# Dense projections of a hybrid decoder: three token blocks of 384, 384, 320 become 256, 416, 416, and the first block multiplies its high and low activations in one product of 512 columns

## The chip, the cores and the metric

The kernel runs on one core of one Trainium2 chip. The metric is the device time of one execution in microseconds. Three runs of the kernel before took 5048.07, 5056.26 and 5062.81 us, so the median is 5056.26 us. One execution was also recorded by the hardware profiler; its span is 5055.9 us.

## The reference, cut to what matters

Two layers of a decoder trunk process 1088 tokens (1024 of a prompt and 8 x 8 of samples), each a row of 1024 numbers in float32.

```
xn   = rmsnorm(x)                       # x * rsqrt(mean(x*x) + eps) * gain
z    = xn @ w_in                        # 1024 -> 2048 mixer columns + 4 * 1024 gate columns
br_a = short convolution, br_b = convolution of width 31 + layer norm,
br_c = pooling windows 2..16, br_d = gated unit on chunks of 128   # each 256 wide, from z
x    = x + (sum_i sigmoid(gate_i) * (br_i @ w_branch_i)) @ w_out
layer 0: x = x + (silu(xn2 @ wg) * (xn2 @ wu)) @ wd          # dense, 2816 wide
layer 1: x = x + top-2-of-8 experts of the same form, 3584 wide
x    = x + sigmoid(rmsnorm(x) @ ple_w_gate) * (p @ ple_w_proj)
```

The result is a last rmsnorm of x and the states of the mixers.

## The kernel before, in words

Activations lie transposed, channels on partitions and tokens along the free dimension. Every number is held as a high and a low part (fp32r) whose sum is the float32 value: `XHI` and `XLO` for the activations, `WHI` and `WLO` for the weights. A product of two such numbers is three products, high x high, high weight x low activation, low weight x high activation (`product`, lines 699 to 708), all added up in one PSUM bank. The share that is not computed is low x low.

A dense unit (`column_unit`) makes 128 output channels for all 1088 tokens. The tokens go in three blocks, `BLOCKS` of 384, 384 and 320. Per block there are 8 slices of the contraction (KC = 8), each with 3 matmuls, so 24 matmuls to a block and 72 to a unit; each block fills one bank of a ring of six. `open_bank` lets TensorE run at most five blocks ahead of the evictions. There are 168 dense units: 46 of the input projection, 8 of `w_out` and 8 of the last gate in each layer, and 44 of the dense feed-forward. The `w_out` units take `MHI` and `MLO`, the merged branches, in place of `XHI` and `XLO`.

The order of the work on each engine is written out by hand, and each engine does its list in that order. Weights are brought in by SyncE's DMA queue, split into a high part by ScalarE (line 1302) and a low part by VectorE (`convert`, line 1703), three units ahead. VectorE takes each block out of PSUM with one `tensor_tensor` that multiplies by the reciprocal norm `RSTD` of the tokens (lines 1824, 1870, 1878, 2100, 2232, 2242), or, for `w_out`, adds to the residual (line 2212).

Four kinds of place matter besides the plain units:

- `gate_project` (TensorE from line 748, VectorE from line 1830) runs eight steps d = 0 to 7, each a dense unit for a gate and three small branch products (lines 754 to 756, 6 matmuls a block). In step 0 the three gate blocks come first and then the three branch products; in the later steps they alternate. Before the first branch product of a step, TensorE waits until VectorE has made the low part of that step's branch weight (`split_pw`, line 1793), which VectorE does in the step before, ahead of the third block. There are five such stages per layer: br_d, br_a, br_b, br_c and the last gate with the projected embedding (here the embedding stage).
- In the embedding stage VectorE, per block, evicts the gate (line 1824), adds a square into the norm (line 1731), multiplies the branch by the gate (line 2585) and adds the two halves of the residual (lines 2588, 2590); ScalarE takes the sigmoid (line 1346) and the squares (line 1646), and converts the next weight only after the third block.
- Norms: after the first block of some units TensorE does other work, handed in as `between`: the sums of squares over channels (line 732), the spread of the reciprocal norm over partitions (line 744), transposes of states (lines 803, 807). Each waits for VectorE first, and TensorE goes on with the second block only after it.
- The first `w_out` unit of a layer takes slice k as soon as VectorE has made `MLO` of slice k (line 1817); four of the eight slices are made only after the last branch product.

The experts of layer 1 and the second half of the feed-forward (`down`, lines 810 to 823) have loops of their own. `down` also goes over `BLOCKS`.

Of the kernel before, what the change touches and what calls it, by code (L numbers as in the profile page):

```python
# [39 lines left out]
BLOCKS = ((0, 384), (384, 384), (768, 320))  # L40
# [98 lines left out]
def build(nc, A, O):  # L139
# [18 lines left out]
    XHI = sb("XHI", [P, KC, NTOK], F32R)  # L158
    XLO = sb("XLO", [P, KC, NTOK], F32R)
# [6 lines left out]
    T = [sb(f"T{i}", [P, 384]) for i in range(4)]  # L166
    IDF = sb("IDF", [P, P])
    IDR = sb("IDR", [P, P], F32R)
    TRIL = sb("TRIL", [P, P])
# [9 lines left out]
    XHF, XLF = XHI[:].bitcast(F32), XLO[:].bitcast(F32)  # L179
# [3 lines left out]
    MLO = at("MLO", [P, KC, NTOK], F32R, PH)  # L183
    MHI = at("MHI", [P, KC, NTOK], F32R, PH + 34816)
# [61 lines left out]
    def mo(name, shape, dt=F32):  # L246
# [85 lines left out]
        "xnew_ready", "y_full", "v_out", "par_ready", "rw_loaded", "nrs_loaded", "rtok_clear", "row_squares", "scale_ready", "ids_ready", "mask_ready", "list_ready", "rows_written", "squared", "summed", "sums_taken", "weights_ready", "spacer")}  # L332
# [78 lines left out]
    def _(sp):  # L411
# [20 lines left out]
        def load_x(block):  # L432
            t0, m = BLOCKS[block]
# [98 lines left out]
    def _(g):  # L532
# [4 lines left out]
        g.memset(IDF[:], 0.0).then_inc(S["pool_own"], 1)  # L537
        g.memset(TRIL[:], 1.0).then_inc(S["pool_own"], 1)
        g.wait_ge(S["pool_own"], 2)
        g.affine_select(out=IDF[:], in_=IDF[:], compare_op=ALU.not_equal, fill=1.0, base=0, pattern=[[-1, P]],  # L540
# [139 lines left out]
    def _(pe):  # L680
# [29 lines left out]
        def blocks_of(HI, LO, splits=None, between=()):  # L710

            slot = unit.n % HL
            for j, (t0, n) in enumerate(BLOCKS):
                b = open_bank()
                product(b, n, slot, lambda k: HI[:, k, t0:t0 + n], lambda k: LO[:, k, t0:t0 + n],
                        (lambda k: splits(j, k)) if splits else None).then_inc(q.next(), 1)
                if j < len(between):
                    between[j]()

        def column_unit(HI, LO, splits=None, between=()):  # L720

            use()
            blocks_of(HI, LO, splits, between)
            unit.n += 1
# [14 lines left out]
        def spread():  # L739

            pe.wait_ge(S["diag_ready"], diag.take())
            for j, (t0, n) in enumerate(BLOCKS):
                b = misc_bank()
                pe.matmul(PS[:, b, 0:n], ONES[:], T[j][:, 0:n], start=True, stop=True).then_inc(m.next(), 1)
# [3 lines left out]
        def gate_project(ready, count, Y, splits=None, between=()):  # L748

            def branch(t0, n):  # L750
                b = open_bank()
                wh, wl = PWH[pw.n % 2], PWL[pw.n % 2]
                for k in range(2):
                    pe.matmul(PS[:, b, 0:n], wh[:, k, :], Y[0][:, k, t0:t0 + n], start=(k == 0), stop=False)  # L754
                    pe.matmul(PS[:, b, 0:n], wh[:, k, :], Y[1][:, k, t0:t0 + n], start=False, stop=False)  # L755
                    ins = pe.matmul(PS[:, b, 0:n], wl[:, k, :], Y[0][:, k, t0:t0 + n], start=False, stop=(k == 1))  # L756
                ins.then_inc(q.next(), 1)

            for d in range(KC):
                use()  # L760
                slot = unit.n % HL
                if d == 0:
                    blocks_of(XHI, XLO, splits, between)
                    pe.wait_ge(S[ready], count)
                    pe.wait_ge(S["pw_lo"], pw.n + 1)
                    for t0, n in BLOCKS:
                        branch(t0, n)
                else:
                    for t0, n in BLOCKS:
                        b = open_bank()  # L770
                        product(b, n, slot, lambda k: XHI[:, k, t0:t0 + n], lambda k: XLO[:, k, t0:t0 + n]).then_inc(q.next(), 1)
                        if t0 == 0:
# [53 lines left out]
        pe.wait_ge(S["consts"], 3)  # L826
# [3 lines left out]
        for block, (t0, n) in enumerate(BLOCKS):  # L830
# [16 lines left out]
        for l in range(DEPTH):  # L847

            def p_columns(tiles):
                pe.wait_ge(S[f"p_loaded{l}"], 16 * NT)  # L850
                for c in range(2):
                    for t0, n in BLOCKS:
                        b = misc_bank()
                        for j in range(t0 // P, -(-(t0 + n) // P)):
                            w = tokens(j)
                            ins = pe.transpose(PS[:, b, j * P - t0:j * P - t0 + w], tiles[j][0:w, c * P:(c + 1) * P], IDF[0:w, 0:w])
                        ins.then_inc(m.next(), 1)

            if l:
                column_unit(XHI, XLO, splits=lambda j, k: W_MIX1 + KC * j + k + 1, between=(stats, spread))  # L860
                column_unit(XHI, XLO)
            else:
                use()
                slot = unit.n % HL
                for j, (t0, n) in enumerate(BLOCKS):
                    pe.wait_ge(S["evicted"], KC * (j + 1))
                    b = open_bank()
                    product(b, n, slot, lambda k: XHI[:, k, t0:t0 + n], lambda k: XLO[:, k, t0:t0 + n]).then_inc(q.next(), 1)
                unit.n += 1
                column_unit(XHI, XLO, between=(spread,))  # L870
# [24 lines left out]
            for _ in range(3):  # L895
                column_unit(XHI, XLO)
# [18 lines left out]
            column_unit(XHI, XLO)  # L915
            gate_project("br_d", l + 1, U_SPLIT, between=(lambda: states_out(GLU, YB, PB),))
            for _ in range(4):
                column_unit(XHI, XLO)
            column_unit(XHI, XLO, between=(lambda: states_out(ZA, YA, PA),))
            column_unit(XHI, XLO)  # L920
# [10 lines left out]
            column_unit(XHI, XLO, between=(channel_sums,))  # L931
            pe.wait_ge(S["lnsq_ready"], l + 1)
            token_sums(SQB[:, 0, :], SQB[:, 1, :])
            column_unit(XHI, XLO, between=(spread,))
# [11 lines left out]
            for d in range(KC):  # L946
                merged = (W_FFN if l == 0 else W_MOE) - 3 * KC - KC
                column_unit(MHI, MLO, splits=(lambda j, k: merged + k + 1) if d == 0 else None)
            if l == 0:
                hs = Count()  # L950

                def step(kind, g, first=False):
                    if kind == "GU":
                        for u in range(4):
                            if first and u == 0:
                                column_unit(XHI, XLO, splits=lambda j, k: W_FFN - 3 * KC + 3 * k + j + 1, between=(stats, spread))
                            else:
                                column_unit(XHI, XLO)
# [296 lines left out]
            else:  # L1255
                gate_project("p_ready", 2, P_SPLIT[1], splits=lambda j, k: hs.at(hs.n + min(6 * j + 6, 2 * NT)), between=(spread,))
# [15 lines left out]
    def _(act):  # L1272
# [110 lines left out]
        for t0, n in BLOCKS:  # L1383
# [8 lines left out]
        for block, (t0, n) in enumerate(BLOCKS):  # L1392
# [298 lines left out]
    def _(dve):  # L1691
# [20 lines left out]

        pending = []
# [35 lines left out]
        def diagonals():  # L1749

            for j, (t0, n) in enumerate(BLOCKS):
# [10 lines left out]
        def spread_rstd():  # L1762

            for t0, n in BLOCKS:
# [54 lines left out]
        def gates(d, j, pulls=0):  # L1819

            t0, n = BLOCKS[j]
            ps = main_ready()
            t = T[j] if d == 0 else T[req.n % 2]
            v.do(dve.tensor_tensor(t[:, 0:n], ps[:, 0:n], RSTD[:, t0:t0 + n], ALU.mult), q)
# [36 lines left out]
        def padded_unit(buf, pad, c, times=False, tmp=[0]):  # L1861

            convert()
            for j, (t0, n) in enumerate(BLOCKS):
                ps = main_ready()
                ps_r = ps
                if times:
                    t = T[2 + tmp[0] % 2]
                    tmp[0] += 1
                    v.do(dve.tensor_tensor(t[:, 0:n], ps[:, 0:n], RSTD[:, t0:t0 + n], ALU.mult), q)  # L1870
# [3 lines left out]
                    v.sync()  # L1874
                else:
                    ds = pieces(j, buf[:, c, :], pad)
# [24 lines left out]
        def p_columns(whole, parts):  # L1901

            for c in range(2):
                for t0, n in BLOCKS:
# [18 lines left out]
        v.do(dve.tensor_copy(IDR[:], IDF[:]))  # L1923
# [13 lines left out]
        for j, (t0, n) in enumerate(BLOCKS):  # L1937
# [16 lines left out]
        for l in range(DEPTH):  # L1954
# [18 lines left out]
            for c in range(2):  # L1973
                convert()
                for t0, n in BLOCKS:
                    ps = main_ready()
                    v.do(dve.tensor_tensor(UB[:, c, t0:t0 + n], ps[:, 0:n], RSTD[:, t0:t0 + n], ALU.mult), q)
# [117 lines left out]
            for c in range(2):  # L2095
                convert()
                for t0, n in BLOCKS:
                    ps = main_ready()
                    t = T[2]
                    v.do(dve.tensor_tensor(t[:, 0:n], ps[:, 0:n], RSTD[:, t0:t0 + n], ALU.mult), q)  # L2100
# [26 lines left out]
            for t0, n in BLOCKS:  # L2127
# [65 lines left out]
            for d in range(KC):  # L2193
# [26 lines left out]
            if l == 0:  # L2220
# [5 lines left out]
                def step(kind, g, last=False):  # L2226
                    if kind == "GU":
                        for f in range(2):
                            convert()
                            for t0, n in BLOCKS:  # L2230
                                ps = main_ready()
                                v.do(dve.tensor_tensor(GS[:, f, t0:t0 + n], ps[:, 0:n], RSTD[:, t0:t0 + n], ALU.mult), q)
                                v.sync()
                                dve.sem_inc(req.next(), 1)
                        for f in range(2):
                            convert()
                            for j, (t0, n) in enumerate(BLOCKS):
                                ps = main_ready()
# [3 lines left out]
                                v.do(dve.tensor_tensor(t, ps[:, 0:n], RSTD[:, t0:t0 + n], ALU.mult), q)  # L2242
# [28 lines left out]
                per = {conv: 12, q: 72, req: 12, split: 12, sreq: 12, v.own: 12}  # L2271
# [386 lines left out]
```

## Time and profile before

| what | value |
|---|---|
| time, three runs | 5048.07, 5056.26, 5062.81 us; median 5056.26 us |
| profiled execution | span 5055.9 us; what lies around the span is not recorded for it, and the median of the runs is 0.4 us above the span |
| TensorE matmul busy | 4935.7 us, 98% of the span, 33281 matmuls |
| VectorE busy | 3231.2 us, 64% |
| ScalarE busy | 1745.1 us, 35% |
| mean granted TensorE clock | 0.987 |

Matmuls of the records overlap: one of 384 columns is shown as 0.33 us long, while the next one starts 0.17 us after it. What a matmul costs in a stream is therefore read from the distance between starts, not from its length. A granted clock of 1.00 is the upper of the two levels, 2.4 GHz; 0.50 is the lower, 1.2 GHz. In rows of the timeline, the bracket at the end tells how long the engine had been idle and what ended it; "DVEq L1795" is VectorE's queue signalling at line 1795.

### The profile page before, as it was taken

Reading aid. Unit: us, or ns where it says so; the run is one execution under the profiler, and the core shown is the slowest. Engines: PE = TensorE matmul, PEld = TensorE weight load, DVE = VectorE, ACT = ScalarE, POOL = GpSimd, SP = SyncE. Lnnn points to the kernel's source line nnn. Section 1 sums busy time; section 2 is a strip of 40 time slices with the busy share of each in tenths; the row PEclk is TensorE's granted clock in tenths of the full one; section 3 lists DMA queues with packets and bytes.
Section 4 is the critical chain, followed back from the end, with each engine's and each line's share of the span. In section 5 each row is a group of like instructions: output and inputs, shape, how many; then the busy total and the mean of one; then the engine's idle time right before and its main releaser. Section 6 shows DMA issues by size and latency. Waiting matters only on the chain.

```text
span 5055.9 us, 87486 instructions
## 1 busy us (share of the span) xinstructions
PE 4935.7 (98%) x33281; PEld 4878.9 (96%) x33282; DVE 3231.2 (64%) x5248; ACT 1745.1 (35%) x2666; POOL 302.4 (6%) x441
## 2 busy tenths in 40 slices
PE   8999999999999999999979999999999999999998
PEld 8999999999998999999979999999999999999988
DVE  4666656444546656766557777666667787876655
ACT  3323322111113433233234444333334444443333
POOL 2000002111112000000020000000000000000030
PEclk9999999999999999999989999999999999999999
DMA  3111111111111111111025554444446555554431
GB/s 107 45 47 41 42 39 42 51 41 41 50 42 44 42 46 52 48 41 42 30 90 197 178 178 165 157 141 161 153 150 197 188 194 186 197 192 153 142 134 43
DMA packets 397853, 521.94 MB, mean 103 GB/s; under 512 B 13192, under 2 KB 353654, under 8 KB 397512
## 3 DMA queue, kind: packets, MB, share of 16 engines
q1 hardware_dynamic: 358320, 459.63, 27.5%
q10 hardware_dynamic: 29272, 33.08, 1.9%
q0 software_dynamic: 9920, 24.85, 1.7%
q8 instruction: 193, 3.16, 0.3%
q14 instruction: 148, 1.21, 0.1%
HBM read 494.91 MB, written 22.60 MB: 102 GB/s over the span
## 4 chain that ended last, share of the span: by engine, by line
PE 81%; issue 9%; DVE 5%; DMA 2%; ACT 1%; DVEq 0%; POOL 0%; ACTq 0%; SPq 0%; POOLq 0%
PE PS L705 20%; PE PS L707 19%; PE PS L706 19%; PE PS L818 5%; PE PS L820 5%; PE PS L819 5%; PE PS L754 1%; PE PS L755 1%; PE PS L756 1%; DMA WRAW<-in_moe_w_gate 1%; DVE EACC L2509 1%; PE PS L1244 1%; DVE WLO L1703 1%; ACT WHI L1302 1%; DVE XSL L2458 0%
## 5 line engine op out<-in xcount | busy, mean ns | idle before, releaser
L1703 DVE TENSOR_TENSOR WLO<-WRAW,WHI 128x1024 fp32r<-128x1024 f32 x866 | 1060.0, 1225 | 417.9 <-ACT WHI L1302 298.3
L705 PE MATMUL PS<-XHI,WHI 128*128 128x384 f32 (+1 forms) x3648 | 1200.9, 329 | 14.4 <-DVE XLO L1960 8.3
L707 PE MATMUL PS<-XHI,WLO 128*128 128x384 f32 (+1 forms) x3648 | 1196.1, 328 | 0.0
L1302 ACT ACTIVATE WHI<-WRAW 128x1024 fp32r<-128x1024 f32 x866 | 899.3, 1051 | 858.8 <-PE PS L820 603.4
L706 PE MATMUL PS<-XLO,WHI 128*128 128x384 f32 (+1 forms) x3648 | 1195.2, 328 | 0.0
L705 PE MATMUL PS<-XSH,WHI 128*128 128x232 f32 (+6 forms) x3584 | 1059.1, 296 | 14.5 <-DVEq L2461 12.0
L707 PE MATMUL PS<-XSH,WLO 128*128 128x232 f32 (+6 forms) x3584 | 1055.6, 295 | 0.0
L706 PE MATMUL PS<-XSL,WHI 128*128 128x232 f32 (+6 forms) x3584 | 1054.1, 294 | 0.0
L705 PEld LDWEIGHTS PS<-XHI,WHI 128*128 128x128 f32 x3648 | 689.9, 189 | 16.6 <-issue 9.0
L705 PEld LDWEIGHTS PS<-XSH,WHI 128*128 128x128 f32 x3584 | 678.8, 189 | 16.6 <-DVEq L2461 13.6
L706 PEld LDWEIGHTS PS<-XLO,WHI 128*128 128x128 f32 x3648 | 689.7, 189 | 0.9
L707 PEld LDWEIGHTS PS<-XHI,WLO 128*128 128x128 f32 x3648 | 689.4, 189 | 0.0
L707 PEld LDWEIGHTS PS<-XSH,WLO 128*128 128x128 f32 x3584 | 679.0, 189 | 0.0
L706 PEld LDWEIGHTS PS<-XSL,WHI 128*128 128x128 f32 x3584 | 678.7, 189 | 0.0
L818 PE MATMUL PS<-EHI,WHI 128*128 128x232 f32 (+6 forms) x1792 | 532.0, 297 | 4.8 <-DVE EACC L2509 3.0
L820 PE MATMUL PS<-EHI,WLO 128*128 128x232 f32 (+6 forms) x1792 | 525.0, 293 | 0.0
L819 PE MATMUL PS<-ELO,WHI 128*128 128x232 f32 (+6 forms) x1792 | 524.5, 293 | 0.0
L2509 DVE TENSOR_TENSOR EACC<-PS,EACC 128x336 f32<-128x336 f32 x832 | 372.7, 499 | 43.1 <-PE PS L820 15.9
L818 PEld LDWEIGHTS PS<-EHI,WHI 128*128 128x128 f32 x1792 | 338.8, 189 | 7.2 <-DVE EACC L2509 3.8
L1346 ACT ACTIVATE T<-T 128x384 f32<-128x384 f32 (+1 forms) x240 | 121.9, 508 | 640.7 <-DVEq L1826 640.4
L819 PEld LDWEIGHTS PS<-ELO,WHI 128*128 128x128 f32 x1792 | 338.9, 189 | 0.0
L820 PEld LDWEIGHTS PS<-EHI,WLO 128*128 128x128 f32 x1792 | 338.8, 189 | 0.0
(408 smaller groups left out, 5810.6 us busy)
## 6 DMA issues: line engine op xcount, KB each, us to landing
WRAW<-in_moe_w_gate SPq DMA_DIRECT2D x112, 1024.0 KB, 5.0
WRAW<-in_moe_w_up SPq DMA_DIRECT2D x112, 1024.0 KB, 5.0
WRAW<-in_moe_w_down SPq DMA_DIRECT2D x112, 1024.0 KB, 4.9
WRAW<-in_w_in SPq DMA_DIRECT2D x48, 1024.0 KB, 5.2
WRAW<-in_ffn_w_gate SPq DMA_DIRECT2D x11, 1024.0 KB, 5.3
WRAW<-in_ffn_w_up SPq DMA_DIRECT2D x11, 1024.0 KB, 5.3
WRAW<-in_ffn_w_down SPq DMA_DIRECT2D x11, 1024.0 KB, 4.9
expert_rows<-YT ACTq DMA_DIRECT2D x18, 512.0 KB, 3.8
```

The lines of the kernel that those rows point to most:

```text
L705: pe.matmul(PS[:, bank, 0:n], wh, hi(k), start=(k == 0), stop=False)
L706: pe.matmul(PS[:, bank, 0:n], wh, lo(k), start=False, stop=False)
L707: ins = pe.matmul(PS[:, bank, 0:n], wl, hi(k), start=False, stop=(k == KC - 1))
L754: pe.matmul(PS[:, b, 0:n], wh[:, k, :], Y[0][:, k, t0:t0 + n], start=(k == 0), stop=False)
L755: pe.matmul(PS[:, b, 0:n], wh[:, k, :], Y[1][:, k, t0:t0 + n], start=False, stop=False)
L818: pe.matmul(PS[:, b, 0:n], WHI[s][:, d, :], hi[:, f, t0:t0 + n], start=(f == 0), stop=False)
L819: pe.matmul(PS[:, b, 0:n], WHI[s][:, d, :], lo[:, f, t0:t0 + n], start=False, stop=False)
L820: ins = pe.matmul(PS[:, b, 0:n], WLO[s][:, d, :], hi[:, f, t0:t0 + n], start=False, stop=(f == 1))
L1302: act.activation(WHI[halves.n % HL][:], raw_view(tile % RAW, half, kind), ACT.Copy).then_inc(halves.next(), 1)
L1346: serve(lambda: act.activation(t[:, 0:n], t[:, 0:n], ACT.Sigmoid))
L1703: v.do(dve.tensor_tensor(WLO[s][:], raw_view(conv.n // 2 % RAW, conv.n % 2, kind), WHI[s][:].bitcast(F32), ALU.subtract), conv)
L2509: v.do(dve.tensor_tensor(a, ps[:, 0:CAP], a, ALU.add), q)
```

## The change

`BLOCKS` becomes 256, 416, 416 for all that is tied to a dense unit, `down` and the branch products included. `TILED` keeps the old cuts for the transposes at the start and for the norms. The high and low activations become the two planes of one tensor (`X2`, and `M2` for `w_out`). In the first block each slice is two matmuls in place of three: the high weight with both planes, 2 x 256 = 512 columns, and the low weight with the high plane, 256 columns, added to that plane's half of the bank. So the bank holds two parts, and VectorE adds them: a `tensor_reduce` over the pair, then the multiplication by `RSTD` in SBUF (`scaled`); for `w_out` two additions. The other blocks are as before, 24 matmuls each. The tiles `T` grow to 416 columns; the identity matrix shares its memory between its two types to make room.

```
-BLOCKS = ((0, 384), (384, 384), (768, 320))
+BLOCKS = ((0, 256), (256, 416), (672, 416))
+TILED = ((0, 384), (384, 384), (768, 320))
+HALF = BLOCKS[0][1]
...
-    XHI = sb("XHI", [P, KC, NTOK], F32R)
-    XLO = sb("XLO", [P, KC, NTOK], F32R)
+    X2 = sb("X2", [P, 2, KC, NTOK], F32R)
+    XHI, XLO = X2[:, 0], X2[:, 1]
...
+        def pair_product(bank, slot, X, hi, splits=None):
+            both = PS[:, bank, 0:2 * HALF].rearrange("p (h t) -> p h t", h=2)
+            for k in range(KC):
+                if splits is not None:
+                    pe.wait_ge(S["split_done"], splits(k))
+                pe.matmul(both, WHI[slot][:, k, :], X[:, :, k, 0:HALF], start=(k == 0), stop=False)
+                ins = pe.matmul(PS[:, bank, hi * HALF:(hi + 1) * HALF], WLO[slot][:, k, :], X[:, hi, k, 0:HALF], start=False, stop=(k == KC - 1))
+            return ins
...
+        def scaled(j, out):
+            t0, n = BLOCKS[j]
+            ps = main_ready()
+            if j == 0:
+                v.do(dve.tensor_reduce(out, ps.rearrange("p (h t) -> p t h", h=2), AXX, ALU.add), q)
+                v.sync()
+                v.do(dve.tensor_tensor(out, out, RSTD[:, t0:t0 + n], ALU.mult))
+            else:
+                v.do(dve.tensor_tensor(out, ps[:, 0:n], RSTD[:, t0:t0 + n], ALU.mult), q)
...
-                    v.do(dve.tensor_tensor(t, ps[:, 0:n], XHF[:, d, t0:t0 + n], ALU.add), q)
+                    if j == 0:
+                        v.do(dve.tensor_tensor(t, ps[:, 0:n], XHF[:, d, t0:t0 + n], ALU.add))
+                        v.sync()
+                        v.do(dve.tensor_tensor(t, ps[:, n:2 * n], t, ALU.add), q)
+                    else:
+                        v.do(dve.tensor_tensor(t, ps[:, 0:n], XHF[:, d, t0:t0 + n], ALU.add), q)
```

## Rows read from the trace of the kernel before

**Rows 1.** The page: busy us (share of the span) and instructions of each engine

```profile
PE 4935.7 (98%) x33281; PEld 4878.9 (96%) x33282; DVE 3231.2 (64%) x5248; ACT 1745.1 (35%) x2666; POOL 302.4 (6%) x441
```

**Rows 2.** Busy time by stretch: PE, PEld, DVE, ACT, POOL, clock, DMA share

```profile
1100.00:1200.00 100.00, 100.00 (x608) 100.00 (x607) 41.70 (x67) 17.37 (x27) 15.45 (x26) 1.00 0.17 52
...
1660.00:1770.00 110.00, 104.57 (x630) 103.53 (x629) 70.38 (x127) 44.64 (x89) 0.00 (x0) 1.00 0.12 38
```

**Rows 3.** Timeline of PE, feed-forward: one dense unit and the next one's start

```profile
1107.17 0.34 PE L705 MATMUL PS<-XHI,WHI 128*128 128x384 f32 x1
...
1115.52 0.31 PE L705 MATMUL PS<-XHI,WHI 128*128 128x320 f32 x1
...
1119.03 0.34 PE L705 MATMUL PS<-XHI,WHI 128*128 128x384 f32 x1
```

**Rows 4.** Timeline of PE: 256 columns read as two ranges of 128, twelve starts

```profile
69.92 0.28 PE L879 MATMUL PS<-WHI,XHI 128*128 128x256 f32 x1
...
71.36 0.28 PE L879 MATMUL PS<-WHI,XHI 128*128 128x256 f32 x1
```

**Rows 5.** Timeline of PE: 512 columns read as four ranges of 128

```profile
4859.16 0.39 PE L1240 MATMUL PS<-XLO,IDR 128*128 128x512 f32 x1
4859.40 0.83 PE L1244 MATMUL PS<-DG,YG 128*128 128x128 f32 x6
```

**Rows 6.** Groups by line of DVE: busy us, mean ns, idle before and releaser

```profile
L1824 DVE TENSOR_TENSOR T<-PS,RSTD 128x384 f32<-128x384 f32 x160 | 88.7, 554 | 86.5 <-PE PS L707 83.4 <-DVE XNEW L2590 1.9 <-DVE T L1824 0.2
...
L1824 DVE TENSOR_TENSOR T<-PS,RSTD 128x320 f32<-128x320 f32 x80 | 39.3, 491 | 68.3 <-PE PS L707 64.6 <-DVE PWL L1793 2.5 <-PE PS L756 0.2
...
L2019 DVE TENSOR_TENSOR V<-V,LNG 128x256 f32<-128x256 f32 x16 | 5.5, 420 | 0.1
...
L2403 DVE TENSOR_REDUCE LROW<-LCMP 14x32 f32<-14x416 f32 x1 | 0.6, 574 | 0.0
```

**Rows 7.** Timeline of DVE, embedding stage of layer 0: last additions of three steps

```profile
1694.49 0.49 DVE L2590 TENSOR_TENSOR XNEW<-XNEW,XLO 128x320 f32<-128x320 f32 x1
...
1711.21 0.49 DVE L2590 TENSOR_TENSOR XNEW<-XNEW,XLO 128x320 f32<-128x320 f32 x1
...
1724.54 0.49 DVE L2590 TENSOR_TENSOR XNEW<-XNEW,XLO 128x320 f32<-128x320 f32 x1
```

**Rows 8.** Waits of DVE from 1662 to 1770: us in total, times, longest

```profile
DVE T L1824 <- PE PS L707: 0.3, 2, 0.2
```

**Rows 9.** Timeline of PE, embedding stage of layer 1: first branch products of steps

```profile
4959.73 0.44 PE L754 MATMUL PS<-PTMHI,PWH 128*128 128x384 f32 x1 [0.57 <-DVEq L1795]
...
4975.41 0.44 PE L754 MATMUL PS<-PTMHI,PWH 128*128 128x384 f32 x1 [0.57 <-DVEq L1795]
```

**Rows 10.** Timeline of DVE up to br_a's and br_b's weight for step 1

```profile
332.14 0.49 DVE L2100 TENSOR_TENSOR T<-PS,RSTD 128x320 f32<-128x320 f32 x1 [1.69 <-PE PS L707]
...
349.94 0.42 DVE L1793 TENSOR_TENSOR PWL<-PWR,PWH 128x256 fp32r<-128x256 f32 x1
...
506.64 0.42 DVE L1793 TENSOR_TENSOR PWL<-PWR,PWH 128x256 fp32r<-128x256 f32 x1
```

**Rows 11.** Timeline of PE: step 1's first branch product, br_a, br_b, br_d

```profile
350.89 0.34 PE L754 MATMUL PS<-YAHI,PWH 128*128 128x384 f32 x1
...
507.18 0.45 PE L754 MATMUL PS<-YBHI,PWH 128*128 128x384 f32 x1
...
1907.64 0.45 PE L754 MATMUL PS<-UHI,PWH 128*128 128x384 f32 x1 [1.27 <-DVEq L1795]
```

**Rows 12.** The chain that ended last, layer 0, at the first w_out unit

```profile
731.99 4.91 DVE MLO L1817 x4
```

**Rows 13.** Timeline of DVE, then PE: last square added, sums of squares, feed-forward

```profile
832.25 0.48 DVE L1731 TENSOR_TENSOR SQS<-SQS,T 128x320 f32<-128x320 f32 x1
...
833.53 2.04 PE L732 MATMUL PS<-ONES,SQS 128*128 128x1 f32 x18
```

**Rows 14.** Timeline of PE, start of layer 1: the spread of the norm

```profile
1786.12 2.37 PE L744 MATMUL PS<-T,ONES 128*128 128x384 f32 x6 [0.89 <-DVEq L1760]
```

More of the change, by code:

```diff
@@ L165, in build @@
     RSTD = sb("RSTD", [P, NTOK])
-    T = [sb(f"T{i}", [P, 384]) for i in range(4)]
-    IDF = sb("IDF", [P, P])
+    T = [sb(f"T{i}", [P, WIDE]) for i in range(4)]
     IDR = sb("IDR", [P, P], F32R)
+    IDF = IDR[:].bitcast(F32)
+    EYE = T[3][:, 0:P]
     TRIL = sb("TRIL", [P, P])
@@ L432, in load_x @@
         def load_x(block):
-            t0, m = BLOCKS[block]
+            t0, m = TILED[block]
             for j in range(t0 // P, -(-(t0 + m) // P)):
@@ L768, in gate_project @@
                 else:
[L769 to L772, printed above, removed]
+                    for j, (t0, n) in enumerate(BLOCKS):
+                        block_of(j, slot, X2, 0)
+                        if j == 0:
                             pe.wait_ge(S["pw_lo"], pw.n + 1)
@@ L829, in _ @@
         pe.transpose(PS[:, b, 0:7 * KC], NRS[:], IDF[0:7 * KC, 0:7 * KC]).then_inc(m.next(), 1)
-        for block, (t0, n) in enumerate(BLOCKS):
+        for block, (t0, n) in enumerate(TILED):
             tiles = range(t0 // P, -(-(t0 + n) // P))
@@ L851, in p_columns @@
                 for c in range(2):
-                    for t0, n in BLOCKS:
+                    for t0, n in TILED:
                         b = misc_bank()
@@ L864, in _ @@
                 slot = unit.n % HL
-                for j, (t0, n) in enumerate(BLOCKS):
+                for j in range(len(BLOCKS)):
                     pe.wait_ge(S["evicted"], KC * (j + 1))
-                    b = open_bank()
-                    product(b, n, slot, lambda k: XHI[:, k, t0:t0 + n], lambda k: XLO[:, k, t0:t0 + n]).then_inc(q.next(), 1)
+                    block_of(j, slot, X2, 0)
                 unit.n += 1
-                column_unit(XHI, XLO, between=(spread,))
+                column_unit(X2, between=(spread,))
             use(2)
@@ L1255, in _ @@
             else:
-                gate_project("p_ready", 2, P_SPLIT[1], splits=lambda j, k: hs.at(hs.n + min(6 * j + 6, 2 * NT)), between=(spread,))
+                gate_project("p_ready", 2, P_SPLIT[1], splits=lambda j, k: hs.at(hs.n + 2 * -(-sum(BLOCKS[j]) // P)), between=(spread,))
         stats()
@@ L1391, in _ @@
         act.wait_ge(S["rtok_clear"], 1)
-        for block, (t0, n) in enumerate(BLOCKS):
+        for block, (t0, n) in enumerate(TILED):
             tiles = range(t0 // P, -(-(t0 + n) // P))
@@ L1749, in diagonals @@
         def diagonals():
-            for j, (t0, n) in enumerate(BLOCKS):
+            for j, (t0, n) in enumerate(TILED):
                 whole = n // P
@@ L1762, in spread_rstd @@
         def spread_rstd():
-            for t0, n in BLOCKS:
+            for t0, n in TILED:
                 ps = misc_ready()
@@ L1903, in p_columns @@
             for c in range(2):
-                for t0, n in BLOCKS:
+                for t0, n in TILED:
                     ps = misc_ready()
@@ L1936, in _ @@
         dve.sem_inc(S["par_ready"], 1)
-        for j, (t0, n) in enumerate(BLOCKS):
+        for j, (t0, n) in enumerate(TILED):
             for c in range(KC):
@@ L2126, in _ @@
             diagonals()
-            for t0, n in BLOCKS:
+            for t0, n in TILED:
                 ps = misc_ready()
@@ L2270, in _ @@
                 cs = [conv, q, req, split, sreq, v.own]
-                per = {conv: 12, q: 72, req: 12, split: 12, sreq: 12, v.own: 12}
+                per = {conv: 12, q: 72, req: 12, split: 12, sreq: 12, v.own: 20}
                 with dve.Fori(0, FFN_LOOP) as i:
```

97 lines of the change are left out of this document (51 added, 46 removed).

## The prediction

> **What bounds the kernel now.** I read the page's busy times first, then stretches, then single units. TensorE is busy 98% of the span and VectorE 64% [rows 1], so the path runs through TensorE unless a stretch says otherwise. In the feed-forward TensorE has no gap in 100 us at the full clock, while VectorE works 42 of them [rows 2]; VectorE's additions are hidden there. In the embedding stage of layer 0 TensorE is busy only 104.6 of 110 us [rows 2], and there VectorE waits for TensorE's products only 0.3 us in all [rows 8]: the chain VectorE to ScalarE and back sets the pace. The reader should keep these two apart, since the change speeds TensorE and slows VectorE.
>
> **What the matmuls cost.** In a dense unit 48 matmuls of 384 columns take 8.35 us, 174.0 ns from start to start, and 24 of 320 take 3.51 us, 146.3 ns; the unit takes 11.86 us [rows 3]. At clock 1.00 (2.4 GHz) a column is 0.4167 ns: 160.0 and 133.3 ns, and 14.0 and 12.9 ns are left. With 256 columns in two ranges of 128, twelve starts take 1.44 us, 120.0 ns, of which 13.3 are left [rows 4]. So a matmul costs its columns plus about 13.3 ns, whatever its width, and reading two ranges costs nothing.
>
> The columns do not change: 8 x (512 + 256) in the first block are the 24 x 256 that it would have had. What changes is the count, 64 matmuls a unit in place of 72. Eight fixed parts are 107 ns. The 512-column matmul isn't in the dense units before; the nearest row, four ranges of 128 and followed by another kind of matmul, shows 0.24 us [rows 5] against 226.7 ns by the rule above. I take 228, near the two-range row since the new read has two ranges; the other end, 240, stays for the range. A unit then costs 8 x 228 + 8 x 120.0 + 48 x 186.7 = 11.74 us against 26112 x 0.4167 + 72 x 13.3 = 11.84: 0.096 us less. By the ends it is 0.107 and 0.000. Sixteen of the 168 units lie in the two embedding stages, which another chain paces (below). The rest give 152 x 0.096 = **14.6 us** gained (0 to 16.2). The second feed-forward half and the branch products keep count and columns: nothing.
>
> The Trainium skill, "TensorE: Matmul & The Clock Gate", section "Back-to-back issue gap", puts the gap of a warm matmul at N / 2.4 ns plus 2.5 ns. By that, 168 x 8 = 1344 matmuls fewer would give 3.4 us. The trace disagrees at these widths (13 to 14 ns). What this would leave is the second rival below.
>
> **What VectorE pays.** An eviction of 384 takes 554 ns, one of 320 491 [rows 6], so 0.984 ns an element, and 416 takes 585 (estimate). A 256-wide multiplication in SBUF takes 420, a reduction of 416 elements 574 [rows 6]; for 512 in PSUM I estimate 668, with 420 (no slower than 256) and 1340 (the two halves, 1 KB apart, read at half rate) as ends. Per unit: before 554 + 554 + 491 = 1.60 us; after 668 + 30 to the dependent start + 420 + 585 + 585 = 2.29: **0.69 us more**, 0.44 to 1.36. ScalarE's sums stay, as all its work is linear in the same 1088 tokens. Where TensorE has no gap this costs nothing; it is paid in these places:
>
> 1. Embedding stage, layer 0. Two steps take 1694.49 to 1724.54, 30.05 us [rows 7]; TensorE would need 2 x (11.86 + 2.96) = 29.6. The chain gate, sigmoid, additions, square, weight conversion and next gate runs without a gap. Seven steps x 0.69 = 4.8. At the start, blocks 1 and 2 stand behind the norm's matmuls and grow by 128 tokens: 24 x 128 x 0.4167 ns = 1.3. Sum **6.1**.
> 2. Embedding stage, layer 1. Steps follow at 15.68 us, and TensorE waits for the branch weight [rows 9]. Four such steps x (0.69 + 0.07 for signals) and 0.4 at step 1: **3.4**. The last steps convert no weight and have slack.
> 3. Step 1 of the mixer stages. VectorE makes the branch weight after three gates, so this wait is the tightest. In br_a it is anchored at the eviction 332.14 that waited for TensorE; the weight is there at 349.94 + 0.42, and TensorE comes at 350.89 [rows 10, 11]: 0.5 us of slack, 0.4 past the signal. TensorE's way from the same anchor gets shorter by 1.5 (block 0 is 2.78 instead of 4.18 us, and 0.1), VectorE's longer by 0.8: a new wait of 1.9 per layer. In br_b the weight comes at 507.06 and TensorE at 507.18 [rows 10, 11], no slack; the anchor lies behind an earlier first block, so TensorE's way shrinks only 0.2, while VectorE's has two reductions: 1.5 per layer. br_d in layer 1 waits already 1.27 [rows 11] and gets 0.8 more, in layer 0 0.7. Sum 3.8 + 3.0 + 1.5 = **8.3**. From step 2 on the weights are several us early; br_c is early throughout. Everything queued behind this wait on TensorE is late with it.
>
> **What the shorter first block uncovers.** TensorE takes its list in order, and some waits are hidden by block 0, which falls from 4.18 to 2.78 us. The squares of the feed-forward norm end at 832.73 and TensorE comes at 833.53 [rows 13]: 0.8 of slack against 1.4 less cover and 0.4 longer chain (416 evicted in place of 320): 1.0. In the first `w_out` unit VectorE makes four slices in 4.91 us [rows 12] while TensorE has only block 0 to do; 128 tokens more are left behind it (1.1) and the chain starts 0.3 later: 1.4 a layer, 2.8. At the start of layer 1 the spread already waits 0.89 [rows 14], and the block behind it grows by 96 tokens: 0.9. The routing of the experts and the end of the kernel hang on a last block that is 416 in place of 320: 0.5 and 0.65. Sum **5.9**. The start of the kernel, the experts and SyncE's and GpSimd's queues are not touched: they use the old cuts.
>
> **Sum.** -14.6 + 6.1 + 3.4 + 8.3 + 5.9 = +9.1 us on the profiled execution's span of 5055.9: **5065 us**, 0.18% more. The median of the three runs, 5056.26, stands 0.4 above that span, so I add nothing for what lies around it. With a measurement that tells about 0.3% (15 us) from no change, the forecast is "no change, a little slower".
>
> **Rivals.**
>
> - *The saving comes whole, the waits do not.* VectorE catches up inside the stages (its background additions are pulled at fixed points and end sooner), and of the 23.7 us of losses only the embedding stage of layer 0 stays. Then 5055.9 - 16.2 + 4.8 = 5044, or 5040 without most of that too. For it: from step 2 on the mixer stages have slack. Against: step 1 comes before it, and rows 7 and 8 show a chain without gaps.
> - *The pair product saves nothing* (the other side: slower). Place: each of the 168 first blocks. If the 512-column matmul costs 240 ns as in rows 5, the eight fixed parts are given back (8 x 13.3) and the losses stand alone: 5055.9 + 23.7 = 5080. It decides from 8 x 5.1 ns on, so from about 233 ns: there the sum passes 15 us over. For it: the only 512-column rows. Against: rows 4, where ranges cost nothing and the fixed part is the same as for narrower ones. By the rule of the Trainium skill above (same page and section) it would be 5076.
> - *The reduction runs at half rate* over its two halves: 0.67 us more a unit, 11 more steps of the embedding stages (7.4) and about as many reductions in the step-1 chains (6): 5078. For it: no row reads pairs so far apart. Against: the 574 ns for 416 elements.
>
> **How the numbers follow.** Forecast 0.50, first rival 0.15, second 0.22, third 0.13. The forecast's own range is 5053 to 5070. Slower by over 0.3% (above 5071): most of the second and third, and 0.02 of the forecast, 0.30. Faster (below 5041): two thirds of the first, 0.10. The rest, 0.60, within. The range 5042 to 5081 takes in the ends of the 512-column price and most of the reduction's.
>
> **What would show it.** Starts of a dense unit 11.74 us apart where TensorE has no gap, 512-column starts 228 ns from the next, reductions near 0.67 us. Step 1's first branch products in br_a, br_b and br_d with VectorE's queue as releaser, together some 8 us more idle. Embedding stage of layer 0 about 5 us longer, 15.7 us a step. A sums-of-squares matmul that waits 1 us in the feed-forward. The prediction is wrong if the 512-column matmul is above 233 ns, if a reduction takes over 1 us, or if the step-1 waits are not there.

## The result, and the profile after

The changed kernel takes 5083.24 us (median of four runs, 5079.87 to 5091.60), the kernel before 5057.59 in the runs beside it: a ratio of 1.0055, 95% interval 1.0043 to 1.0066. It is slower by 25.7 us. The forecast was 5065, with a range that ends at 5081. The profiled execution of the changed kernel has a span of 5078.3 us, 22.4 more than before.

The page's busy times after:

```profile
PE 4941.6 (97%) x31937; PEld 4801.9 (95%) x31938; DVE 3333.7 (66%) x5416; ACT 1744.7 (34%) x2666; POOL 295.3 (6%) x441
```

Against [rows 1] TensorE has exactly the 1344 matmuls fewer that the change promised, and is busy 5.9 us *more*. VectorE pays 102.5 us. So matmuls have gone, but not their time. Where it stayed is seen in a stretch of the feed-forward without gaps. The timeline of PE after, two dense units: first matmul of the first block, of the second block, and of the next unit.

```profile
1113.65 0.40 PE L720 MATMUL PS<-X,WHI 128*128 128x512 f32 x1
...
1116.43 0.35 PE L709 MATMUL PS<-X,WHI 128*128 128x416 f32 x1
...
1125.50 0.39 PE L720 MATMUL PS<-X,WHI 128*128 128x512 f32 x1
...
1128.31 0.36 PE L709 MATMUL PS<-X,WHI 128*128 128x416 f32 x1
...
1137.42 0.40 PE L720 MATMUL PS<-X,WHI 128*128 128x512 f32 x1
```

The two units take 11.85 and 11.92 us; before it was 11.86 [rows 3], the forecast 11.74. The first blocks take 2.78 and 2.81 us, as forecast (8 x 348 ns = 2.78). The 48 matmuls of 416 columns take 9.07 and 9.11 us, 189.0 and 189.8 ns each, where 186.7 was forecast. That is most of the difference; in the second unit the first block gives another 0.03.

VectorE's groups by line after (busy us, mean ns, idle before); L1738 adds the halves, L1740 multiplies, L1742 evicts 416 columns:

```profile
L1742 DVE TENSOR_TENSOR T<-PS,RSTD 128x416 f32<-128x416 f32 x228 | 134.8, 591 | 215.6 <-PE PS L711 206.3 <-DVE PWL L1824 3.5 <-DVE XNEW L2623 2.3
...
L1738 DVE TENSOR_REDUCE T<-PS 128x256 f32<-128x512 f32 x114 | 78.0, 684 | 1.5 <-PE PS L721 1.1 <-DVE XNEW L2623 0.4
...
L1740 DVE TENSOR_TENSOR T<-T,RSTD 128x256 f32<-128x256 f32 x114 | 48.8, 428 | 4.0
```

684, 428 and 591 ns stand against 668, 420 and 585 of the estimate. Three waits of PE after (total us, times, longest), to be read beside [rows 9 to 14]:

```profile
PE PS L776 <- DVEq L1826: 13.3, 11, 2.2
...
PE PS L720 <- DVE M L1848: 5.6, 8, 1.6
...
PE PS L754 <- DVEq L2253: 1.0, 1, 1.0
```

L776 is the first branch product behind its weight, L720 the first `w_out` units, L754 the sums of squares of the feed-forward norm. The wait of the branch products was, before:

```profile
PE PS L754 <- DVEq L1795: 4.0, 5, 1.3
```

It grew as forecast, but mostly elsewhere: of the 13.3 us after, 4.5 are at step 1 of br_a, br_b and br_d (1.27 before) and 8.8 in the embedding stages (2.75 before). At step 1 some 8 us more were forecast, and 3.2 came.

### The profile page after: what moved, and what is told of

Same layout as the page of the kernel before. It is cut to its first block, busy times and chain, and to the rows that moved or that the text cites. A ratio compares the mean times of both kernels' runs of the same rounds, so it can differ in the third digit from the quotient of the medians.

```text
span 5078.3 us, 84998 instructions
## 1 busy us (share of the span) xinstructions
PE 4941.6 (97%) x31937; PEld 4801.9 (95%) x31938; DVE 3333.7 (66%) x5416; ACT 1744.7 (34%) x2666; POOL 295.3 (6%) x441
## 4 chain that ended last, share of the span: by engine, by line
PE 48%; issue 8%; DVE 4%; DMA 2%; ACT 1%; DVEq 0%; POOL 0%; ACTq 0%; POOLq 0%; SPq 0%
PE PS L709 10%; PE PS L710 10%; PE PS L711 10%; PE PS L839 3%; PE PS L840 3%; PE PS L841 3%; PE PS L720 2%; PE PS L721 1%; PE PS L776 1%; PE PS L1264 1%; PE PS L778 1%; PE PS L777 1%; DMA WRAW<-in_moe_w_gate 1%; DVE EACC L2542 0%; DMA WRAW<-in_moe_w_up 0%
## 5 line engine op out<-in xcount | busy, mean ns | idle before, releaser
L709 PE MATMUL PS<-X,WHI 128*128 128x416 f32 x2432 | 860.0, 354 | 0.0
L710 PE MATMUL PS<-X,WHI 128*128 128x416 f32 x2432 | 856.1, 352 | 0.0
L711 PE MATMUL PS<-X,WLO 128*128 128x416 f32 x2432 | 855.3, 352 | 0.0
L709 PEld LDWEIGHTS PS<-X,WHI 128*128 128x128 f32 x2432 | 458.9, 189 | 8.3 <-issue 0.6
L710 PEld LDWEIGHTS PS<-X,WHI 128*128 128x128 f32 x2432 | 458.9, 189 | 4.9 <-issue 0.6
L711 PEld LDWEIGHTS PS<-X,WLO 128*128 128x128 f32 x2432 | 458.7, 189 | 4.4
L720 PE MATMUL PS<-X,WHI 128*128 128x512 f32 x1216 | 442.4, 402 | 14.8 <-DVE X L1992 7.5
L2542 DVE TENSOR_TENSOR EACC<-PS,EACC 128x336 f32<-128x336 f32 x832 | 373.4, 500 | 42.9 <-PE PS L841 15.8
L1366 ACT ACTIVATE T<-T 128x416 f32<-128x416 f32 (+1 forms) x240 | 121.7, 507 | 659.8 <-DVEq L1856 659.5
L721 PE MATMUL PS<-X,WLO 128*128 128x256 f32 x1216 | 345.2, 284 | 0.0
```

The costliest lines, as they stand in the source:

```text
L709: pe.matmul(PS[:, bank, 0:n], wh, hi(k), start=(k == 0), stop=False)
L710: pe.matmul(PS[:, bank, 0:n], wh, lo(k), start=False, stop=False)
L711: ins = pe.matmul(PS[:, bank, 0:n], wl, hi(k), start=False, stop=(k == KC - 1))
L720: pe.matmul(both, WHI[slot][:, k, :], X[:, :, k, 0:HALF], start=(k == 0), stop=False)
L721: ins = pe.matmul(PS[:, bank, hi * HALF:(hi + 1) * HALF], WLO[slot][:, k, :], X[:, hi, k, 0:HALF], start=False, stop=(k == KC - 1))
L1366: serve(lambda: act.activation(t[:, 0:n], t[:, 0:n], ACT.Sigmoid))
```

## The experiments

The table gives the time from the first matmul of one dense unit to that of another, read from the timeline of PE of one profiled execution each, in us. "Adds" is VectorE's addition of the halves.

| stretch | before | after | e1 cuts alone | e2 three + adds | e3 pair, no adds | e4 pair last | e7 pair hidden |
|---|---|---|---|---|---|---|---|
| two feed-forward units | 23.72 | 23.77 | 23.92 | 23.92 | 23.77 | 23.77 | 23.77 |
| first `w_out` unit, layer 0 | 15.05 | 18.40 | 18.61 | 18.80 | 18.89 | 15.33 | 15.34 |
| the same, layer 1 | 16.07 | 18.68 | 18.49 | 18.97 | 19.13 | 15.35 | 15.35 |
| first feed-forward unit | 16.08 | 17.27 | 18.90 | 18.84 | 20.39 | 17.58 | 17.54 |
| br_a, step 1, layer 0 | 14.84 | 16.64 | 15.83 | 16.57 | 15.88 | 16.26 | 14.97 |
| br_b, step 1, layer 0 | 15.00 | 15.44 | 14.85 | 15.45 | 14.84 | 15.90 | 15.60 |
| embedding stage, layer 0, steps 1 to 7 | 113.11 | 118.76 | 113.38 | 118.78 | 113.36 | 120.23 | 114.32 |
| embedding stage, layer 1, steps 0 to 6 | 112.67 | 116.02 | 113.19 | 116.23 | 113.20 | 115.93 | 112.13 |
| experts (code unchanged) | 2338.44 | 2339.28 | 2344.99 | 2336.68 | 2342.73 | 2341.56 | 2336.38 |

The last row varies by 8.6 us among kernels with the same code there; medians are not fine enough to read a single term from them, the stretches are.

**e1, the cuts alone.**

```
-            if j == 0:
-                ins = pair_product(b, slot, X, hi, splits)
-            else:
+            if True:
                 t0, n = BLOCKS[j]
                 ins = product(b, n, slot, ...)
```

and the same for VectorE's addition.

> The changed kernel's blocks of 256, 416, 416, but with 24 ordinary matmuls of 256 in the first block and no addition on VectorE. It isolates the cuts. The trace of the changed kernel shows starts 118.7 ns apart at 256 columns, 189.1 at 416 and 232.6 at 512; the line through 256 and 512 is 4.8 ns + 0.445 ns a column, and 264, 288, 312, 328, 336 and 416 columns lie within 1 ns of it. Theory L (a matmul costs by its columns at 0.445 ns and only 4.8 ns besides): three blocks of any widths cost the same, so a dense unit takes 11.86 to 11.93 us as before, and what is lost is what the shorter first block uncovers, without VectorE's additions: some 11 us (4.5 at the first w_out units with their clock, 1.8 at step 1 of br_a, 1.3, 1.1, 1.0, 0.8, 0.8 at the other places): about 5069 us. Theory F of the prediction (13.3 ns a matmul, 0.4167 ns a column): unit 11.84, the same 5069. Rival W (the width 416 is dear by itself): units 0.07 to 0.12 us longer, 152 of them: 5080 to 5087.

Measured: 5086.55 us, ratio 1.0057 (1.0043 to 1.0071). Two units' starts in the feed-forward, timeline of PE:

```profile
1117.87 0.28 PE L709 MATMUL PS<-X,WHI 128*128 128x256 f32 x1
...
1141.79 0.28 PE L709 MATMUL PS<-X,WHI 128*128 128x256 f32 x1
```

23.92 us for two: 11.96 a unit, 0.10 more than before with the same columns and the same 72 matmuls. So theory L, which I had read out of the trace of the changed kernel after the result, falls, the prediction's flat 13.3 ns (F) falls with it, and rival W stands as far as the units go: these cuts with 416 columns cost by themselves. e5 below shows that the width alone doesn't make the price. The expected 5069 was missed. The rows of the embedding stages are back to within 0.6 us of before: what was lost there is VectorE's addition. br_a's step 1 keeps 1.0 of its 1.8 us (the shorter first block), and 0.8 goes with the addition. The first `w_out` units keep their loss. The first feed-forward unit takes 1.6 us longer than in the changed kernel: its granted clock is at half for some 3.3 us (0.89 from 840 to 855 us; 1.00 in the changed kernel).

**e2, three matmuls of 256 into the two halves, with the addition.**

```
-                pe.matmul(both, WHI[slot][:, k, :], X[:, :, k, 0:HALF], start=(k == 0), stop=False)
+                pe.matmul(part(hi), WHI[slot][:, k, :], X[:, hi, k, 0:HALF], start=(k == 0), stop=False)
...
+                ins = pe.matmul(part(1 - hi), WHI[slot][:, k, :], X[:, 1 - hi, k, 0:HALF], ...)
```

> The changed kernel, but in the first block the 512-column matmul is replaced by two of 256 columns into the two halves of the bank; VectorE adds the halves as in the changed kernel. 72 matmuls a unit again. It isolates the count. Theory L: 8 x (3 x 118.7 - 350.1) = 0.05 us more a unit, 152 units outside the embedding stages: 7 us slower than the changed kernel, about 5090. Theory F: 8 x 13.3 ns = 0.107 us a unit, 16 us slower, 5099. Rival (the 512-column matmul costs as much as two): no difference, 5083.

Measured: 5095.28 us, ratio 1.0081 (1.0068 to 1.0095). 41.0 us above its runs of before, where the changed kernel is 25.7 above its own: 15 us, with some 6 of uncertainty on each. The units say it more sharply: 23.92 against 23.77 for two, 0.075 a unit, between L (0.05) and F (0.107). The pair product does save time; 152 units make 11.4 us.

**e3, the pair product without the addition.** The product of the high weight and the low activation stays in the bank and out of the result.

```
-            if j == 0:
-                v.do(dve.tensor_reduce(out, ps.rearrange("p (h t) -> p t h", h=2), AXX, ALU.add), q)
...
+            if True:
                 v.do(dve.tensor_tensor(out, ps[:, 0:n], RSTD[:, t0:t0 + n], ALU.mult), q)
```

> The changed kernel, but VectorE takes only one half of the first block's bank out (the half that holds both products of the high activation; the product of the high weight and the low activation is left out of the result), with one multiplication as before. It isolates VectorE's additions. If the prediction's terms for VectorE hold (4.8 in the embedding stage of layer 0, 3.4 in that of layer 1, and of step 1's 8.3 the part that is not the shorter block, some 3): 11 us faster than the changed kernel, about 5072. If the additions are hidden and the losses are the cuts' alone: 5083.

Measured: 5074.49 us, ratio 1.0037 (1.0025 to 1.0049); about 5 us less against its own runs of before than the changed kernel, where 11 were expected. By stretches the expectation holds: 5.4 and 2.8 us in the embedding stages, 0.8 and 0.6 at step 1 of br_a and br_b in layer 0. Its experts took 3.5 us longer than the changed kernel's, its first feed-forward unit 3.1 and its first `w_out` units 0.9. In the first feed-forward unit the clock accounts for it: 0.77 from 832 to 847 us, 1.00 in the changed kernel, so 6.9 us at half, worth 3.4. The waits of PE:

```profile
PE PS L776 <- DVEq L1822: 6.3, 9, 1.0
```

6.3 us for 13.3: half of that wait goes with the addition.

**e4, the short block last.**

```
-BLOCKS = ((0, 256), (256, 416), (672, 416))
+BLOCKS = ((0, 416), (416, 416), (832, 256))
+PAIR = 2
```

> Blocks of 416, 416, 256 with the pair product and VectorE's addition in the last block. Same matmuls in every unit as the changed kernel, but the first block is longer than before (24 x 189 = 4.54 us for 4.18) and covers the norms, the first w_out unit and step 1. Theory L with losses from the cover: the uncovered places and their low clock are gone (about 14 us of the changed kernel's 25.6), step 1's waits shrink by some 2 us, VectorE's additions in the embedding stages stay (8 us), units as in the changed kernel: 5062 us, 5057 to 5067. Theory F: 5050, since the units would gain their 14.6 us as well. If the order of the blocks doesn't matter: 5083.

Measured: 5073.46 us, ratio 1.0035 (1.0022 to 1.0049), 19.1 above before. The cover is given back where expected: the first `w_out` units are at 15.33 and 15.35. But the first feed-forward unit still loses (17.58 us for 16.08 before, 17.27 after; the clock is 0.89 from 835 to 850 us), step 1 of br_a and br_b still loses (16.26 and 15.90), and the embedding stage of layer 0 grew to 120.23. So the order of the blocks was worth 6.4 us in the first `w_out` units (against after) and 2.5 in the embedding stage of layer 0 with its step 0 and the start of layer 1 together, and nothing in the units; the expected 5062 was missed, since it took nearly all losses but VectorE's in the embedding stages for covered.

**e5, the price by width.** A program of its own: 48 matmuls of each width, like those of a block.

> Nothing of the reference is computed: streams of matmuls like a block's (24 with the weights of 8 slices, two products with the high and one with the low weight, all into one bank), of 128 to 512 columns, first with no other engine at work, then with VectorE and ScalarE busy in SBUF. It measures the price of a matmul by width, by itself. Theory L: 4.8 ns + 0.445 ns a column: 256 columns 118.7 ns, 320 147, 384 176, 416 190, 448 204, 480 218, 512 233, whether one range or two planes 34.8 KB apart, and in both stretches. Theory F: 13.3 ns + 0.4167 ns: 120, 147, 173, 187, 200, 213, 227. Rival (the steeper slope comes of the other engines' reads and writes): by F in the quiet stretch, by L in the busy one. Rival (the two planes cost): 2 x 256 some 6 ns above one range of 512.

Measured: no difference between the quiet and the busy stretch. First matmul of each stream of 48, timeline of PE, quiet stretch; the distance of two streams' first rows by 48 is the price. 139.38 is the 25th of 512 columns; 165.45 is the first of 24 that read two planes of 256; from 170.94 on come pair products:

```profile
81.50 0.31 PE L129 MATMUL PS<-X,WHI 128*128 128x320 f32 x1
...
88.54 0.32 PE L129 MATMUL PS<-X,WHI 128*128 128x352 f32 x1
...
96.22 0.34 PE L129 MATMUL PS<-X,WHI 128*128 128x384 f32 x1
...
104.54 0.35 PE L129 MATMUL PS<-X,WHI 128*128 128x416 f32 x1
...
113.58 0.36 PE L129 MATMUL PS<-X,WHI 128*128 128x448 f32 x1
...
123.49 0.38 PE L129 MATMUL PS<-X,WHI 128*128 128x480 f32 x1
...
133.89 0.40 PE L129 MATMUL PS<-X,WHI 128*128 128x512 f32 x1
...
139.38 0.39 PE L129 MATMUL PS<-X,WHI 128*128 128x512 f32 x1
...
144.82 0.35 PE L129 MATMUL PS<-X,WHI 128*128 128x416 f32 x1
...
153.78 0.28 PE L146 MATMUL PS<-X,WLO 128*128 128x256 f32 x1
...
165.45 0.40 PE L146 MATMUL PS<-X,WLO 128*128 128x512 f32 x1
...
170.94 0.39 PE L138 MATMUL PS<-X,WHI 128*128 128x512 f32 x1
...
173.75 0.40 PE L138 MATMUL PS<-X,WHI 128*128 128x512 f32 x1
```

320, 352 and 384 columns cost 146.7, 160.0 and 173.3 ns (the last is 104.54 - 96.22 by 48): 13.3 above 0.4167 ns a column. 512 costs 227.7, 14.4 above. Those are theory F's numbers, nearly so at 512 (226.7). But 416 costs 188.3 (15.0 above), 448 costs 206.5 (19.8), 480 costs 216.7 (16.7). Theory L fails here. And the width alone doesn't set the price: two more blocks of 416, behind the 512 and reading the tokens from 256 and from 672 as the kernel's blocks do, take 8.96 us (144.82 to 153.78), 186.7 ns each, the price by F. Both figures come again in the busy stretch. In the units of the kernel and of e6, where they follow a block of 256 columns, blocks of the same tokens take 188 to 190. What the price hangs on besides the width was not tested further. The last two rows are eight slices of the pair product: 2.81 us, 351 ns a slice; three of 256 at 120.0 are 360. It saves 9 ns of the 13.3. Two planes as one read of 512 cost what one range of 512 does (the first 24 matmuls take 5.49 us in either stream), so the planes are not dear; in the pair the 512 is followed 236 ns later, its 256 only 117.

**e6, whole units, nothing else at work.**

> Nothing of the reference is computed: streams of matmuls with no other engine at work, first single widths between those measured (264 to 504 columns in steps of 8 to 40), then whole dense units, four of each kind: 384/384/320; 256/416/416, 256/320/512 and 256/352/480, each with an ordinary first block and with the pair product. The widths alone showed 13.3 ns over the columns at 256, 320, 352, 384 and 512, but 13.3 to 15.0 at 416, 20.0 at 448, 16.8 at 480, and a pair at 352.7 ns for three 256-column matmuls at 360.0. Theory W (price by width, dear at 416 to 480; the pair saves 7 ns a slice): units of 11.86 for 384/384/320; 11.93 ordinary and 11.87 with the pair for 256/416/416; 11.85 and 11.79 for 256/320/512; 11.9 and 11.85 for 256/352/480. Theory F of the prediction: 11.84, 11.84 and 11.74 whatever the cut. Theory L (a slope of 0.445 ns and 4.8 ns fixed) has already failed: 320 and 384 lie 13.3 above their columns; it would give 11.97 for every ordinary cut.

Measured, first matmul of each kind, four units apart, timeline of PE: 384/384/320; 256/416/416 ordinary, then pair; 256/320/512 ordinary, then pair; 256/352/480 ordinary, then pair.

```profile
196.43 0.34 PE L113 MATMUL PS<-X,WHI 128*128 128x384 f32 x1
...
243.84 0.28 PE L113 MATMUL PS<-X,WHI 128*128 128x256 f32 x1
...
291.68 0.40 PE L122 MATMUL PS<-X,WHI 128*128 128x512 f32 x1
...
339.22 0.28 PE L113 MATMUL PS<-X,WHI 128*128 128x256 f32 x1
...
386.66 0.39 PE L122 MATMUL PS<-X,WHI 128*128 128x512 f32 x1
...
433.86 0.28 PE L113 MATMUL PS<-X,WHI 128*128 128x256 f32 x1
...
481.81 0.40 PE L122 MATMUL PS<-X,WHI 128*128 128x512 f32 x1
```

By four: 11.85, 11.96, 11.89, 11.86, 11.80, 11.99 us; the last kind, 256/352/480 with the pair, takes 11.87. This is the kernel's own table (11.86, 11.96 in e1, 11.885 after) with no other engine running: the unit's price is TensorE's alone. 256/320/512 with the pair product would save 0.06 a unit against before. It was not tried in the kernel: its four `T` tiles of 512 columns need 1.5 KB a partition more, and the tiles of 416 had already taken the room that was made.

**e7, the pair product only where VectorE is hidden.**

```
-                        block_of(j, slot, X2, 0)
+                        block_of(j, slot, X2, 0, pair=(ready != "p_ready" and d > 1))
```

and an ordinary product in step 0, with e4's blocks. `ready != "p_ready"` leaves out the embedding stages, `d > 1` step 1 of the mixer stages.

> Blocks of 416, 416, 256, the pair product and its addition in the last block, but an ordinary product in the two embedding stages and in steps 0 and 1 of the mixer stages, where VectorE's chain sets the pace. If the losses of the kernel with the pair in the last block are VectorE's chain there (10.4 us in the steps of the embedding stages, some 2 to 4 at step 1) and the price of 416 columns (everywhere, 0.08 us a unit where the pair is taken back, 32 units, 2.6 us): 5073 - 13 + 3 = 5063 us, still slower than before. If the losses in these stages come from the order of the blocks instead: 5073 to 5076.

Measured: 5060.43 us, ratio 1.0007 (0.9997 to 1.0016): no difference from before. The embedding stages are back at 114.32 and 112.13 us, so e4's loss there was the addition, not the order of the blocks. The largest losses are gone (smaller ones stay: the first feed-forward unit 1.5 us, step 1 of br_b 0.6) and the pair's saving is spent on the blocks of 416, so about nothing is left on either side. No version tried beats the kernel before.

## Why the prediction was wrong, point by point

Predicted terms against the same stretches of the profiled executions (after minus before, us):

| term | predicted | measured |
|---|---|---|
| dense units | -14.6 (152 units) | -0.8 (the 118 units in stretches without other terms; predicted for these -11.3) |
| embedding stage, layer 0 | +6.1 | +6.8 (steps 1 to 7 +5.65, step 0 +1.16) |
| embedding stage, layer 1 | +3.4 | +3.4 |
| step 1 of the mixer stages | +8.3 | +4.0 (br_a 1.80 + 1.73, br_b 0.44 + 0.44, br_d 0.58 - 0.98) |
| uncovered by the shorter block | +5.9 | +10.0 (first `w_out` 3.35 + 2.62, feed-forward 1.20, layer 1 1.17, experts 0.84, end 0.83) |
| first units of br_b | none | -3.1 (-1.6 and -1.5) |
| start, and end of the feed-forward | none | +2.2 |

But for rounding, the right column adds up to the 22.4 us between the two spans. The first row alone, 13.8 us off, accounts for the miss of 13.3 (22.4 for 9.1). That the four losses add up to 24.2 for 23.7 is luck: step 1 came 4.3 short, and the uncovered waits 4.1 over, in good part through the clock (below).

**The step that failed** is "So a matmul costs its columns plus about 13.3 ns, whatever its width", used at 416. It held at every width it was taken from (256, 320, 384) and, alone, nearly at 512 (14.4). At 416 the fixed part is 15.7 and 16.5 in the two feed-forward units shown above (189.0 and 189.8 ns), at least 2.4 ns more than taken, 48 times a unit: 0.115 us, more than the whole saving of 0.096. Alone it was 15.0 in one pair of blocks and 13.3 in another (e5), so the rule gave a price that 416 can have, but not the one that it has in these units. Nothing in the prediction bounded that price: the estimate 186.7 for 416 stood without ends, although no row of before had that width, while the ends were spent on the 512-column matmul. The trace of before could have given ends. Its experts have streams of other widths, 24 matmuls between two rows, timeline of PE before:

```profile
2648.11 0.28 PE L705 MATMUL PS<-XSH,WHI 128*128 128x264 f32 x1
...
2651.03 0.28 PE L705 MATMUL PS<-XSH,WHI 128*128 128x264 f32 x1
...
4532.76 0.31 PE L705 MATMUL PS<-XSH,WHI 128*128 128x328 f32 x1
...
4536.38 0.31 PE L705 MATMUL PS<-XSH,WHI 128*128 128x328 f32 x1
```

264 columns take 121.7 ns and 328 take 150.8: 11.7 and 14.2 over their columns. By 14.2 the saving of a unit is 0.05 us, half of what was forecast. The 512-column matmul cost 231 to 233 ns with a following 256 at 117 to 119: 350 a pair for 348 in the sum. By e1 and e2 the change's two halves are +0.10 us a unit for the cuts and -0.075 for the pair.

**The second rival** gave nearly the right time (5080 for a span of 5078.3 and a median of 5083.24) with half the right reason, and so partly by luck: nothing was saved in the units, but not because the 512-column matmul costs 240 ns. Its threshold of 233 ns was nearly met; by e2 the pair product still saves. The first rival falls with the saving. The third falls too: the reduction took 684 ns, near the 668 of the forecast and far from 1340.

**Step 1** was mis-sized at br_b and br_d. br_a came as worked out: a wait of 1.57 us at the branch product for 1.9. Timeline of PE, layer 0:

```profile
353.22 0.39 PE L776 MATMUL PS<-YAHI,PWH 128*128 128x256 f32 x1 [1.57 <-DVEq L1826]
```

br_b had 1.5 predicted and got 0.44, and e3, without the addition, none; the estimate charged two reductions to a chain with no slack, and which part of that was too much was not tested. br_d of layer 1 waited 1.27 before [rows 11]; that stretch became 0.98 shorter.

**The embedding stage** went nearly as read. Last additions of two steps that lie two apart, timeline of DVE after, beside [rows 7]:

```profile
1705.15 0.59 DVE L2623 TENSOR_TENSOR XNEW<-XNEW,X 128x416 f32<-128x416 f32 x1
...
1737.26 0.59 DVE L2623 TENSOR_TENSOR XNEW<-XNEW,X 128x416 f32<-128x416 f32 x1
```

Two steps take 32.1 us for 30.05; 31.4 was forecast. e1 and e3, with no addition, are both at 113.4 for the seven steps. These two steps lost 1.0 us each where 0.69 was forecast, all seven 5.65 for 4.8. Not all of the loss need be the chain: behind a new wait of 2.21 us at a branch product the granted clock fell too (0.89 from 1750 to 1765 us). How much that cost was not tested.

**The first `w_out` unit** lost 3.35 and 2.62 where 1.4 and 1.4 were worked out. Three of the four waits, timeline of PE in layer 0 (the fourth is 0.20):

```profile
734.82 0.50 PE L720 MATMUL PS<-M,WHI 128*128 128x512 f32 x1 [1.62 <-DVE M L1848]
...
736.02 0.78 PE L720 MATMUL PS<-M,WHI 128*128 128x512 f32 x1 [0.59 <-DVE M L1848]
...
737.22 0.79 PE L720 MATMUL PS<-M,WHI 128*128 128x512 f32 x1 [0.21 <-DVE M L1848]
```

From the second on the matmuls are 0.78 us long: the clock has fallen to half behind the wait of 1.62. By windows of 15 us (PE, PEld, DVE, ACT, POOL busy, granted clock, DMA) from 735 on: after, then before, then e4:

```profile
735.00:750.00 15.00, 14.01 (x56) 12.29 (x57) 7.59 (x11) 3.67 (x7) 0.00 (x0) 0.77 0.22 71
```

```profile
735.00:750.00 15.00, 14.18 (x83) 13.54 (x83) 9.28 (x15) 4.34 (x8) 0.00 (x0) 1.00 0.22 71
```

```profile
735.00:750.00 15.00, 14.22 (x73) 12.97 (x74) 9.96 (x15) 4.97 (x9) 0.00 (x0) 1.00 0.22 71
```

A mean of 0.77 over 15 us is 6.9 us at half, worth 3.4: about the whole loss, while the four waits together grew by 0.6 only (2.6 us for 2.0). Before, in layer 0, the waits were 0.78 and three of 0.41, and the clock stayed; in e4, with 24 matmuls of 416 in the first block, the first wait was 1.23 and it stayed too. But the length of the first wait doesn't settle it: in layer 1 before, the waits began with 0.79, 0.41 and 0.41 again, and there the clock did fall. Layer 1, before and then after:

```profile
2482.00:2497.00 15.00, 14.59 (x77) 13.89 (x77) 8.37 (x14) 4.57 (x8) 0.00 (x0) 0.89 0.21 71
```

```profile
2497.00:2512.00 15.00, 14.22 (x60) 12.86 (x59) 6.97 (x12) 2.33 (x5) 0.00 (x0) 0.77 0.22 71
```

So that unit took 16.07 us before, 1.0 more than in layer 0, and lost less by the change. The prediction priced the wait and not what the clock does behind it, though the trace of before had one such case.

The same is behind the unforeseen gain in br_b's first units. Windows from 465 to 480, before and then after:

```profile
465.00:480.00 15.00, 14.54 (x77) 13.47 (x76) 4.24 (x13) 5.83 (x11) 0.00 (x0) 0.77 0.20 67
```

```profile
465.00:480.00 15.00, 14.53 (x83) 13.00 (x82) 5.61 (x16) 5.74 (x11) 0.00 (x0) 0.89 0.22 70
```

0.77 and 0.89 of 15 us are 6.9 and 3.3 us at half; the difference, 3.6 us, is worth 1.8, about the 1.6 gained. In e1 the clock is 0.77 again there, and its first br_b units take what they did before (0.1 less). Why the stretch at half is shorter in the changed kernel stays open.

## What to carry to other kernels

A price per instruction that fits three sizes is not yet a rule for a fourth: give every new size its own bounds, or keep to sizes the trace has. Measure whole units in the order in which they will run, since the price of one width can differ between two streams (here 186.7 and 188.3 ns at 416 columns), and do so before counting instructions saved. And price a new wait on TensorE with the stretch at half clock that can follow it: in the first `w_out` unit of layer 0 that stretch cost more than the wait.

## What the runs showed of the hardware that was not expected

The fixed part of a matmul of this kind (fp32r, high and low weights in turn) does not rise or fall steadily with its width. From e5 and e6, alone, in streams of 48, over 0.4167 ns a column: 10.0 ns at 264, 11 to 12 at 288 and 304, 13.3 to 13.5 at 256, 320, 336, 352, 368, 384, 400, 424 and 496, 14.1 at 392, 14.4 at 512, 15.0 at 408 and 416 (13.3 at 416 behind 512), 15.8 at 432, 16.5 to 16.7 at 376, 440, 464, 480 and 504, 18.3 at 456, 19.8 at 448, 22.6 at 488. VectorE and ScalarE busy in SBUF changed none of those that were measured both ways. At the narrow end the price no longer falls with the width: 232, 192 and 128 columns cost 112.0, 112.3 and 110.6 ns. A width was measured behind one other width only, but for 416, so what belongs to the width and what to the order is open.
